# Second attention of a two-block transformer kernel: the next head's query and key pairs are made ahead of the exponential and of the later masking, and the first rotation of queries runs on VectorE

## What is computed

```python
def latent_attention(h, pos, w_in, q_norm, kv_norm, w_uq, w_ukv, q_gain, k_gain, w_out):
    c_q, c_kv, k_rope = jnp.split(h @ w_in, [256, 384], axis=-1)
    q = (rmsnorm_2(c_q, q_norm) @ w_uq).reshape(B, S, 16, 96)
    kv = (rmsnorm_2(c_kv, kv_norm) @ w_ukv).reshape(B, S, 16, 128)
    k_nope, v = jnp.split(kv, [64], axis=-1)
    k = jnp.concatenate([k_nope, k_rope broadcast over the heads], axis=-1)
    q, k = rmsnorm_2(q, q_gain), rmsnorm_2(k, k_gain)
    # the last 32 of 96 columns of q and k are rotated by the position (apply_rope)
    s = einsum('bqhd,bshd->bhqs', q, k) * 96 ** -0.5      # causal: masked above the diagonal
    o = softmax(s) @ v
    return o.reshape(B, S, 1024) @ w_out
```

## Time and profile before

| | before |
|---|---|
| median of 3 runs | 2756.39 us (2755.81 to 2759.79) |
| profiled execution | 2753.66 us |
| its span | 2752.4 us |
| PE busy | 2683.5 us, 97% |
| DVE, ACT, POOL busy | 1460.3, 972.6, 333.4 us |
| chain that ended last | PE 85%, DVE 8%, ACT 4%, issue 1%, POOL 1% |

### The profile page before, as it was taken

The page is one execution under the profiler, slowest core; times in us unless marked ns, Lnnn a source line. Parts: engine busy times, 40 slices in busy tenths (PEclk is TensorE's granted clock), DMA queues, the critical chain, the costliest instruction groups (busy, mean ns, idle before and its releaser), DMA issues.

```text
span 2752.4 us, 32221 instructions
## 1 busy us (share of the span) xinstructions
PE 2683.5 (97%) x13207; PEld 2251.1 (82%) x13207; DVE 1460.3 (53%) x2298; ACT 972.6 (35%) x1603; POOL 333.4 (12%) x398
## 2 busy tenths in 40 slices
PE   6899999999999999999999999999999989999999
PEld 5788888888877888888888888888888788888887
DVE  4635546655657545555675343544444677443433
ACT  3334334333354212224653232332222477432221
POOL 2000000000012000004550000000000487300000
PEclk9999999999999999999999999999999999999999
DMA  4222233623232275637323323232322200223321
GB/s 141 97 96 84 80 105 119 198 92 107 66 103 78 91 107 76 107 94 118 100 73 107 107 92 99 85 108 94 105 93 77 64 32 32 92 92 99 101 89 64
DMA packets 281194, 258.99 MB, mean 94 GB/s; under 512 B 40516, under 2 KB 276055, under 8 KB 281047
## 3 DMA queue, kind: packets, MB, share of 16 engines
q1 hardware_dynamic: 281047, 256.93, 32.5%
HBM read 242.23 MB, written 14.68 MB: 93 GB/s over the span
## 4 chain that ended last, share of the span: by engine, by line
PE 85%; DVE 8%; ACT 4%; issue 1%; POOL 1%; SPq 0%; DMA 0%; DVEq 0%; POOLq 0%; ACTq 0%
PE bank L1086 27%; PE bank L1088 27%; PE bank L1087 27%; DVE Wl L1763 2%; PE bank L1232 1%; PE bank L1097 1%; ACT Wh L1424 1%; DVE TMP L1956 1%; DVE TMP L1953 1%; DVE TMP L1832 1%; ACT TMP L1537 0%; DVE Pl L1751 0%; PE bank L1283 0%; DVE bank L1821 0%; POOL TMP L2279 0%
## 5 line engine op out<-in xcount | busy, mean ns | idle before, releaser
L1086 PE MATMUL bank<-Hh,Wl 128*128 128x512 f32 x2144 | 843.2, 393 | 8.1 <-DVE Hl L1779 8.1
L1088 PE MATMUL bank<-Hh,Wh 128*128 128x512 f32 x2144 | 837.1, 390 | 0.0
L1087 PE MATMUL bank<-Hl,Wh 128*128 128x512 f32 x2144 | 836.7, 390 | 0.0
L1424 ACT ACTIVATE Wh<-RAW 128x1024 fp32r<-128x1024 f32 (+2 forms) x454 | 441.2, 1022 | 453.1 <-PE bank L1088 399.4
L1763 DVE TENSOR_TENSOR Wl<-RAW,Wh 128x1024 fp32r<-128x1024 f32 (+2 forms) x420 | 494.3, 1220 | 152.4 <-ACT Wh L1424 151.9
L1086 PE MATMUL bank<-Ph,Wl 128*128 128x512 f32 x1200 | 473.4, 394 | 12.7 <-ACT TMP L1471 4.2
L1086 PEld LDWEIGHTS bank<-Hh,Wl 128*128 128x128 f32 x2144 | 403.4, 188 | 95.2 <-DVE Wl L1763 5.0
L1087 PEld LDWEIGHTS bank<-Hl,Wh 128*128 128x128 f32 x2144 | 403.6, 188 | 85.3 <-issue 1.7
L1088 PEld LDWEIGHTS bank<-Hh,Wh 128*128 128x128 f32 x2144 | 403.2, 188 | 85.7
L1087 PE MATMUL bank<-Pl,Wh 128*128 128x512 f32 x1200 | 469.6, 391 | 0.0
L1088 PE MATMUL bank<-Ph,Wh 128*128 128x512 f32 x1200 | 469.4, 391 | 0.0
(11 more groups left out here) (298 smaller groups left out, 2499.5 us busy)
## 6 DMA issues: line engine op xcount, KB each, us to landing
RAW<-in_ffn_wg SPq DMA_DIRECT2D x44, 1024.0 KB, 5.1
RAW<-in_ffn_wu SPq DMA_DIRECT2D x44, 1024.0 KB, 5.1
RAW<-in_ffn_wd SPq DMA_DIRECT2D x32, 1024.0 KB, 5.1
RAW<-in_w_up SPq DMA_DIRECT2D x22, 1024.0 KB, 5.1
RAW<-in_w_in SPq DMA_DIRECT2D x20, 1024.0 KB, 5.1
RAW<-in_ffn_wd SPq DMA_DIRECT2D x16, 768.0 KB, 4.3
bias_scratch<-M SPq DMA_DIRECT2D x16, 512.0 KB, 8.0
RAW<-in_w_down SPq DMA_DIRECT2D x8, 1024.0 KB, 5.3
```

Source lines behind the costliest of these rows:

```text
L1086: mm(o, ll, rh, start=start, stop=False)
L1087: mm(o, lh, rl, start=False, stop=False)
L1088: return mm(o, lh, rh, start=False, stop=stop)
L1424: run(Wh[:, n % 3, x:y], RAW[:, n % 2, x:y], ACT.Copy).then_inc(*w_hi.up(("w_hi", n, i)))
```

## The change

In the loop of `attend_b_order` the masking becomes a step of its own, `b_soft` h, part, on DVE alone, while `b_scores` stays on PE alone. The order within an iteration was, with the engines that have work in each step: scores and masking of part 0, exponential of part 0, low part of turned part 1 of head t, scores and masking of parts 1 and 2, then `b_qk` of head i + 1. It is now: scores of all parts, masking of part 0, low part of turned part 1, `b_qk` of head i + 1 for queries and keys, exponential of part 0, masking of parts 1 and 2. Besides, the rotation of queries for pair 0, which stands before the loop, is emitted by DVE and no longer by POOL, with the same five operations; those of the other pairs stay on POOL.

```diff
         for part in range(3) if i < 16 else ():
             scored.take(("b_s", i, part))
             do("b_scores", i, part)
-            if part == 0:
-                do("b_exp", i, 0)
-                if 0 <= t:
-                    do("b_pt_lo", t, 1)
-        if t in (14, 15):
+        if i < 16:
+            do("b_soft", i, 0)
+        if 0 <= t < 16:
             do("b_pt_lo", t, 1)
         if i < 15:
             for e in range(2):
                 head_qk(i + 1, e)
+        if i < 16:
+            do("b_exp", i, 0)
+            for part in (1, 2):
+                do("b_soft", i, part)
...
-            elif kind == "b_scores":
+            elif kind == "b_rotate":
+                g, = s
+                if g:
+                    continue
...
+                tt(t0, q[:, :, :, 64:96], c_, ALU.mult)
+                tt(t1, q[:, :, :, 80:96], s_[:, :, :, 0:16], ALU.mult)
+                tt(t2, q[:, :, :, 64:80], s_[:, :, :, 16:32], ALU.mult).then_inc(
+                    *dve_out.up(("b_rot_products", g)))
+                dve.wait_ge(*at(("b_rot_products", g)))
+                tt(q[:, :, :, 64:80], t0[:, :, :, 0:16], t1, ALU.add)
+                tt(q[:, :, :, 80:96], t0[:, :, :, 16:32], t2, ALU.add).then_inc(*dve_out.up(("b_rot", g)))
+            elif kind == "b_soft":
...
             elif kind == "b_rotate":
                 g, = s
+                if g == 0:
+                    continue
```

More of the change, by code:

```diff
@@ L2204, in dve_program @@
                     *pair_lo.up((done, h), free=(name, h)))
-            elif kind == "b_scores":
+            elif kind == "b_rotate":
+                g, = s
+                if g:
+                    continue
+                q = qts[g % 2]
+                t0 = pki[:, 128:384].bitcast(F32).rearrange("p (n h d) -> p n h d", n=4, h=2)
+                t1, t2 = (x.rearrange("p (n h d) -> p n h d", n=4, h=2) for x in (krt[:, :], M[:, 7, 384:512]))
+                c_, s_ = (table_of(0, i).unsqueeze(2).broadcast_to([128, 4, 2, 32]) for i in range(2))
+                dve.wait_ge(*at("b_krot"))
+                dve.wait_ge(*at(("b_uqk", g, 1)))
+                dve.wait_ge(*at("rotations"))
+                tt(t0, q[:, :, :, 64:96], c_, ALU.mult)
[6 more added lines that the diff above has]
+            elif kind == "b_soft":
                 h, part = s
```

## The result

The changed kernel takes 2762.78 us (median of 20 runs, 2759.25 to 2767.78) against 2757.43 us of the kernel before (20 runs beside them, 2754.15 to 2761.27). The ratio is 1.0021, with a 95% interval from 1.0015 to 1.0027: slower by 5.3 us, and 1 lies outside the interval. The forecast was 2757.6 with a range of 2751.5 to 2764.0, and a time above 2761.9 had a chance of 0.12. The change itself was forecast at +1.2 us, so it came out more than four times as large; a further 1.0 us lies in the kernel before, which ran at 2757.43 here and at 2756.39 when the forecast was made.

A forecast was written before the change was run, and what follows sets the result against it. PE, busy 97%, was taken as the bound, with 9.1 + 0.6 us of waits as target. +1.5 us for six pairs and -0.34 at the start gave +1.2 on the median 2756.39: 2757.6 us, range 2751.5 to 2764.

The forecast's parts named there:

- Odd iterations: Iteration 7 as example: queries' low part comes before later maskings, removing 1.08 us of PE's wait ahead of the unit.
- what is late next: Odd iterations: turned part 0 ends later, so PE's wait moves from the unit to the turns ahead of the values.
- nothing is gained: Iteration 7: the unit would start at 2266.5, where it started at 2266.55 before.
- The term for a pair: One even and one odd iteration: +0.25 us, bounds 0 to +0.4; six pairs make +1.5 us.
- Even iterations: ACT stalls before its late exponentials until DVE's maskings end, adding 1.05 us to the chain the odd iteration shortens.
- Rival 2: Iterations 1, 3, 5, 9: bunched PE waits lower the clock, each fall at most 1.5 us; chance 0.12 for three or more.
- idle time as dense as in iteration 1: Threshold for a clock fall: 0.97 us busy of 3, as in the stretch 2211.5 to 2214.5.
- From iteration 12 on nothing changes: End of the loop: no unit runs, PE has no such wait and ACT has room, so no time changes.
- Start: Before the loop: the rotation on DVE lets the first scores start 0.34 us sooner, bounds 0 to -0.63.
- with no one waiting: Start: the first keys' low part and next units' sums move by 1.3 us on DVE without delaying anything.
- Rival 1: Whole loop: ACT avoids the stall, all eight waits go, 10.5 to 11 us gained, 2745.5 us; chance 0.09, half gain 0.09.
- Rival 3: Pairs behind iteration 4: keys' turn waits for POOL, up to 1 us in each of four pairs, 2761.6 us; chance 0.04.

The follow-up runs named there:

- e4: Changed kernel, with PE repeating the scores of part 2 in heads 5 and 9 to stay busy; 2757.06 us against 2755.05 before, ratio 1.0009.
- e2: Changed kernel's new loop order, but with the rotation of pair 0 back on POOL; 2759.4 us against 2755.05 before, ratio 1.0015.
- e3: Kernel before, with the new loop order in odd iterations only and the rotation on POOL; 2753.27 us against 2755.05, ratio 0.9992.
- e5: Kernel before, with the new loop order in even iterations only and the rotation on POOL; 2766.62 us against 2757.35, ratio 1.0035.
- e6: Kernel before, with only ACT's order changed (both high parts ahead of the first exponential), DVE's low parts still behind the maskings; 2758.4 us against 2757.35.
- e7: Kernel before, with only the next head's queries moved ahead, in odd iterations, keys behind the maskings, rotation on POOL; 2750.76 us against 2757.35.
- e1: Kernel before with its old loop order, only the rotation of pair 0 moved to DVE; 2755.55 us against 2755.05, ratio 1.0002.
- e10: Kernel before, with only queries moved ahead in odd iterations, plus the rotation of pair 0 on DVE; 2752.2 us against 2757.36, ratio 0.9979.

## Why the prediction was right in its mechanism and short in its size

The time fell inside the range, but the sum did not foresee it: +1.2 us was forecast and +5.3 measured, and the range, from 6 us below the forecast to 6 above, was wide enough to hold both. In the profile the 6.16 us up to the last head are 0.05 at the start (forecast -0.34), 1.03 in iterations 0 and 1, 0.24 in 2 and 3, 2.84 for the order itself from head 4 to 12 (by e4, which keeps the clock; 1.57 of it in the pair of 10 and 11) and 2.0 for the clock.

**Odd iterations and "what is late next": right, with a term somewhat too small.** The wait left the unit and came back ahead of the turn and the product of values, with the releasers named. In iteration 7 the first unit starts 13.48 us behind the scores of head 6 and did so after 13.52 before, which is the "nothing is gained" of the prediction. The term for a pair was 0.25, from 0 to 0.4. The changed kernel's own pair of 6 and 7 has -0.09, but it stands behind a fall of the clock and gets some of it back; where the clock had not fallen, e2 has 0.44 and 0.32 a pair and e4 0.47, 0.32 and 0.48. So the term was mis-sized by 0.1 to 0.2 us a pair, up to iteration 9. One part of it is visible alone: of the odd exponentials' delay 0.2 to 0.7 us was to go on to the next even iteration, and in e3, where nothing covers it, it is 1.0.

**Even iterations: right.** 1.05 us were forecast for the way from the scores to the unit on ACT, 1.20 measured: ACT begins the high parts 0.33 us later than it began the exponential before (0.35 forecast), with DVE's wait of 0.49 (0.5), and the gap on ACT is 0.85 (0.7). e5 and e6 confirm the parts: the even half alone costs 1.2 us and more a pair, ACT's order only 0.2 to 0.33 of it.

**The clock: the right two places, and a wrong weight.** Rival 2 named iterations 5 and 9 and 1.5 us for a fall; measured were 1.48 and 1.38 (1.88 and 1.77 less the 0.40 and 0.39 of e4). What failed is that I kept the sum at no fall, by the argument that it takes idle time as dense as in iteration 1 (0.97 us busy of 3). The clock fell in iteration 5 behind 1.57 us busy of 3, which is less idle time, and in e2 it stayed behind 1.62. With two falls at the prediction's own price the sum would have been 2760.6; net of what comes back, 2.0 us, it would have been 2759.6.

**Iteration 11: a term that was missing.** "From iteration 12 on nothing changes" was right, but at the end of iteration 11 the first output product follows the units and takes the bank of the first, which ACT frees by its copy (L1654). The late exponentials of head 11 push that copy: 1.01 us of wait, and 1.2 us from head 11 to head 12. The prediction let ACT's idle time take up 1.1 us of the delay in odd iterations, and did not ask who else waits there. e3, which delays these exponentials too, has the same wait of 1.00; e7, which delays them half as much, has none.

**Start: wrong, by a small term.** The rotation took 1.35 us on DVE, as priced, and PE's wait for it went. But the 0.34 us did not come. I wrote that the sums of squares behind it move "with no one waiting". The row of ACT in the changed kernel shows who does:

```profile
2198.17 0.49 ACT L1650 ACTIVATE TMP<-bank 128x384 f32<-128x384 f32 x1 [0.97 <-DVE pkf L2190]
```

The square of the next unit needs a buffer of TMP that the sum behind the rotation frees (2198.14); it starts at 2198.17, where 2197.67 would be its time of before in this profile. The high part of the queries follows it and is as late as it was. That the buffer is the cause is read from this row and from e1 and e10, which both start head 0 at +0.02 and +0.05; it was not tried with another buffer.

**Iteration 1: open in part.** By head 2 the changed kernel had lost 1.1 us, e2 3.4 and e4 nothing, all with the new order; the loop of before stood at 0 and 1.2 (e1). The forecast gave these iterations the same 0.25. The new order bunches the waits there too, 2.69 us in front of the turns and 0.50 of clock behind it, but where the clock falls at the start varies by itself (in e1, with the old order, as well), and one profile of each kernel doesn't tell the means apart.

**Rival 1** (the gain stands) falls by the table; about half of the 10.5 to 11 us that it hoped for exists, and e7 takes it, by moving less. **Rival 3** (POOL becomes the releaser) did not come; no wait of L1099 for L2406 appears.

## What to carry to other kernels

Work moved ahead on an in-order engine to cut a wait is work moved behind for everything that stood there, so follow what is pushed back through every engine until it meets the end of its own chain. Here moving half as much, in half the iterations, was worth some 12 us more than the whole (e7 at -6.6 us to before, 2750.76 less 2757.35, and the changed kernel at +5.3). When waits of TensorE move together, price the clock with them: as much idle time in one place can cost more than spread (iterations 5 and 7 of e5), and repeating 3 us of useless products in the idle time (e4) kept the clock at 1.00, though the medians show its gain only just.

## What the runs showed of the hardware

The granted clock does not fall each time that the same queue waits in the same way: with the same loop, iteration 5 went to 0.50 in the changed kernel and stayed at 1.00 in e2, behind waits of 1.29, 0.45 and 0.49 us in the first and 1.27, 0.45 and 0.49 in the second, while iteration 9 (1.93 us and two short ones) fell in both. The Trainium skill (TensorE: Matmul & The Clock Gate, What's actually happening) has the rate depend on recent activity; the runs agree, and what decides at iteration 5 stays open.

The rotation on DVE ran beside POOL's norm, both reading SBUF. No instruction waited for another's end: DVE's multiplications took 0.28 to 0.42 us, and POOL's small ones were stretched, from 0.20 to 0.25 and 0.33 (first row undisturbed, then those beside the rotation):

```profile
2190.43 0.20 POOL L2387 TENSOR_TENSOR pkf<-pkf 128x8 f32<-128x8 f32 x1
...
2195.89 0.25 POOL L2385 TENSOR_TENSOR pkf<-pkf 128x8 f32<-128x8 f32 x1 [3.26 <-DVE pkf L2190]
2196.22 0.33 POOL L2387 TENSOR_TENSOR pkf<-pkf 128x8 f32<-128x8 f32 x1
2196.63 1.68 POOL L2389 TENSOR_TENSOR pkf<-pkf,sm 128x8 f32<-128x8 f32 x1
...
2195.67 0.42 DVE L2218 TENSOR_TENSOR pki<-M,ropt 128x256 f32<-128x256 f32 x1
2196.73 0.29 DVE L2224 TENSOR_TENSOR M<-pki,M 128x128 f32<-128x128 f32 x1
```

The last of DVE's rows lies inside POOL's power of 1.68 us (2196.63 to 2198.31) and takes its usual 0.29. This agrees with the earlier trace rows and not with an exclusive hold of the shared port for a whole instruction (Trainium skill, SBUF — State Buffer, Who interferes with whom), at least for POOL instructions this small.
